# Starting the first supertile after eight of 24 modulation chunks, with the other 16 read beside its attention

## What is computed

```python
mod = c @ ada_w[l] + ada_b[l]                        # (B, 6D)
sh1, sc1, g1, sh2, sc2, g2 = jnp.split(mod, 6, axis=-1)
h = rmsnorm(x, norm1_g[l]) * (1.0 + sc1) + sh1       # needs sh1, sc1 alone
x = x + g1 * token_mixer(h, ...)                     # g1: after the mixer
h = rmsnorm(x, norm2_g[l]) * (1.0 + sc2) + sh2       # needs sh2, sc2
x = x + g2 * hier_moe(h, ...)
# in the mixer, compressed keys and values of 32-token blocks:
blocks = blocks + pos
kc = gelu(flat(blocks) @ w1 + b1) @ w2
```

## Time and profile before

| | |
|---|---|
| median of 3 runs | 6014.1 us (5986.19 to 6021.75) |
| the profiled execution | 5981.45 us |
| its slowest core's span (core 3) | 5979.9 us |
| spans of the 8 cores | 5889.1 to 5979.9 us |
| PE, DVE, ACT, POOL busy on core 3 | 66%, 41%, 34%, 16% |

### The profile page before, as it was taken

How to read it: one execution, slowest core, us unless ns; L and a number is a source line. 1 busy time by engine, 2 the same in 40 slices (tenths; PEclk the granted TensorE clock), 3 DMA queues, 4 the chain that set the end, 5 groups by cost and what they waited for, 6 DMA issues and landing times.

```text
span 5979.9 us, 101776 instructions; the slowest of 8 cores (5889.1 to 5979.9 us)
## 1 busy us (share of the span) xinstructions
PE 3965.3 (66%) x35620; PEld 2453.9 (41%) x35620; DVE 2446.7 (41%) x5534; ACT 2025.3 (34%) x3831; POOL 929.0 (16%) x876
## 2 busy tenths in 40 slices
PE   2477686775777766778687687865289998981000
PEld 1234353343444433344343344432167777771000
DVE  1245444364454444445445445533222222323444
ACT  0234344333354532435443244551011111112332
POOL 2001101011111001101100011001122333322222
PEclk9778778787787877878888778877599999995555
DMA  9567565556755456466564643212265545557886
GB/s 166 135 132 153 112 134 101 127 138 121 124 112 113 116 131 134 106 135 126 107 128 126 130 110 92 71 61 58 81 225 196 203 169 194 186 190 219 250 249 214
DMA packets 212104, 848.33 MB, mean 142 GB/s; under 512 B 37197, under 2 KB 42829, under 8 KB 198808
## 3 DMA queue, kind: packets, MB, share of 16 engines
q1 hardware_dynamic: 147960, 603.37, 32.2%
q0 software_dynamic: 63648, 238.47, 23.5%
HBM read 1218.00 MB, written 285.00 MB: 251 GB/s over the span
## 4 chain that ended last, share of the span: by engine, by line
PE 53%; DMA 17%; DVE 13%; issue 6%; POOL 5%; ACT 4%; another core or an unknown queue 1%; DVEq 1%; ACTq 0%; SPq 0%; POOLq 0%
PE bank L290 45%; DMA ring_u<-wst 8%; DMA xg_u<-h2s,gidu_u 5%; PE bank L293 3%; POOL wl_u L308 3%; PE ACCA L290 2%; DVE wl_u L311 2%; PE ACCB L290 2%; DMA ring_u<-ada_wc 2%; DMA ring_u<-wch 1%; DVE wl_u L308 1%; ACT wl_u L296 1%; POOL h2t_u L308 1%; DVE tmp_u L308 1%
## 5 line engine op out<-in xcount | busy, mean ns | idle before, releaser
L290 PE MATMUL bank<-h1T_u,ring_u 128*128 128x512 bf16 x3072 | 956.8, 420 | 435.6 <-DMA ring_u<-wst 390.1
L296 ACT ACTIVATE pe_u<-bank 128x512 bf16<-128x512 f32 x1648 | 950.5, 598 | 660.1 <-PE ACCB L290 305.5
L290 PE MATMUL bank<-xT_u,wl_u 128*128 128x128 bf16 x10368 | 632.6, 224 | 1.0 <-issue 0.6
L290 PEld LDWEIGHTS bank<-xT_u,wl_u 128*128 128x128 bf16 x10368 | 613.6, 101 | 1.7 <-issue 1.4
L290 PEld LDWEIGHTS bank<-h1T_u,ring_u 128*128 128x128 bf16 x3072 | 297.1, 107 | 718.9 <-issue 548.5
L308 POOL TENSOR_TENSOR rv_u<-rv_u,mhalf_u 128x1 f32<-128x1 f32 x128 | 84.1, 661 | 2920.0 <-DVE rv_u L305 2919.9
L290 PE MATMUL bank<-qz_u,ksr_u 128*128 128x512 bf16 x1088 | 469.5, 432 | 15.8 <-ACT pe_u L296 15.8
L290 PEld LDWEIGHTS ACCA<-vsr_u,pe_u 128*128 128x128 bf16 x4352 | 313.6, 108 | 263.6 <-issue 107.8
L290 PE MATMUL bank<-wores_u,mixT_u 128*128 128x512 bf16 x1024 | 362.1, 418 | 70.1 <-DVE tmp_u L308 43.0
L308 DVE TENSOR_TENSOR he_u<-sg_u,bank 128x512 bf16<-128x512 bf16 x162 | 111.3, 687 | 633.3 <-PE bank L290 556.9
L290 PE MATMUL ACCA<-vsr_u,pe_u 128*128 128x65 bf16 x4352 | 346.0, 206 | 12.0 <-ACT osel_u L299 5.1
(11 more groups left out here) (269 smaller groups left out, 6417.4 us busy)
## 6 DMA issues: line engine op xcount, KB each, us to landing
wl_u<-wsc SPq DMA_DIRECT2D x162, 3072.0 KB
ring_u<-wst SPq DMA_DIRECT2D x390, 512.0 KB
wsc<-exp_all POOLq DMA_DIRECT2D x64, 1536.0 KB, 18.9
wl_u<-yks SPq DMA_DIRECT2D x128, 512.0 KB, 7.8
xs_u<-x SPq DMA_DIRECT2D x64, 512.0 KB
x_u<-x SPq DMA_DIRECT2D x64, 512.0 KB
x1s<-x_u SPq DMA_DIRECT2D x64, 512.0 KB, 3.0
wl_u<-x1s SPq DMA_DIRECT2D x64, 512.0 KB, 6.3
```

The source lines that it names most:

```text
L290: P.emit('pe', lambda e: e.matmul(out, lhsT, rhs, start=start, stop=stop, skip_group_check=True), rd, wr)
L296: P.emit('act', lambda e: e.activation(out=out, in_=in_, func=func, **kw), rd, wr)
```

## The change

The head now ends after the constants that eight modulation chunks need; the rest moves.

- **Head.** DVE clears first. POOL loads `cT`, `identb` and the four ring slots; SP loads the first two x tiles and its constants. Then the barrier, which leaves out the ring slots and the x tiles. Behind it POOL issues 25 loads: 11 constants, four pieces of `vcaug`, and the rows of `ksr` in ten pieces where there were two. Then follow modulation chunks 0 to 7 and `d1(0)`.
- **`biasc`.** The eight `w1` chunks are no longer read for it alone. In `d1(0)` their matmuls with `posT` stand beside the compression ones, in `bank3`.
- **`modgen`** is a new generator woven with `d1(1)` in phase 0. Its first step issues the four `wores` loads (POOL), the copy of `ebase`, the clearing of `fill` and the 18 stores to `idt` (SP); then come modulation chunks 8 to 23, one to a step, all in `bank3`, through the same ring.
- Four small tiles stay allocated, and the x loads of `d1(0)` are no longer issued behind the barrier.

```diff
-    def barrier(self):
+    def barrier(self, skip=()):
...
+                if s in skip:
+                    continue
...
-            for q in range(4):
-                DMA('pool', wores[q][:], wch_d[27 + q][:, 0:2048], 'cst_pool', (), [wores[q]])
...
-            DMA('pool', ksr[0][64:128, :], e40_d, 'cst_pool', (), [ksr[0]])
-            DMA('pool', ksr[1][0:64, :], e40_d, 'cst_pool', (), [ksr[1]])
-            MS(fill[:], PAD, fill)
-            nfill = ROWS // 128
-            for f in range(nfill):
-                DMA('sp', idt_d[f * 128:(f + 1) * 128, :], fill[:], 'fill', [fill], [('idt', 'fill', f)])
+            DMA('pool', cT[:], cT_d, 'l_cT', (), [cT])
+            DMA('pool', identb[:], identf_d, 'l_idb', (), [identb])
+            for c in range(NR):
+                R.warm(c)
+            for q in range(2):
+                DMA('sp', xs[q][:], x_d[q * 128:q * 128 + 128, :], f'xl{q}', (), [xs[q]])
...
+            P.barrier(skip=[f'ring{i}' for i in range(NR)] + ['xl0', 'xl1'])
+            late = [(posT, posT_d), (ptcur, ptcur_d), (ptfirst, ptfirst_d), (ptprev, ptprev_d), (poolw, poolw_d), (w2sb, w2r_d),
+                    (maskD, maskD_d), (maskW, maskW_d), (selvalid, selv_d), (selbiasc, selb_d), (tri, tri_d)]
+            for n_, (dst, src) in enumerate(late):
+                DMA('pool', dst[:], src, f'lt{n_}', (), [dst])
+            for p in range(2):
+                for g in range(2):
+                    DMA('pool', vcaug[p][:, g, 64:97], ovl_d, f'lo{p}{g}', (), [vcaug[p]])
+            for m in range(5):
+                o_ = m * 512
+                DMA('pool', ksr[0][64:128, o_:o_ + 512], e40_d[:, o_:o_ + 512], f'le0{m}', (), [('ks', 0, m)])
+                DMA('pool', ksr[1][0:64, o_:o_ + 512], e40_d[:, o_:o_ + 512], f'le1{m}', (), [('ks', 1, m)])
...
+            def modgen():
                 for q in range(4):
-                    ci, w = R.get(adac(8 + q4 * 4 + q))
...
+                    DMA('pool', wores[q][:], wch_d[27 + q][:, 0:2048], f'lw{q}', (), [wores[q]])
+                P.emit('dve', lambda e: e.tensor_copy(out=base[1][:, 4, :], in_=ebase[:]), [ebase], [base[1]])
+                MS(fill[:], PAD, fill)
+                for f in range(ROWS // 128):
+                    DMA('sp', idt_d[f * 128:(f + 1) * 128, :], fill[:], 'fill', [fill], [('idt', 'fill', f)])
+                bk = banks[3]
+                for q4 in range(4):
+                    mr, br = mrow[q4 % 2], brw[q4 % 2]
+                    DMA('sp', br, adabr_d[:, q4 * D:(q4 + 1) * D], f'brwl{q4 % 2}', (), [br])
+                    for q in range(4):
+                        ci, w = R.get(adac(8 + q4 * 4 + q))
+                        wv = V3(w[:, 0:2048], 8)
+                        for k in range(8):
+                            MM(bk[0:nseq, 0:256], cT[:, k, :], wv[:, k, :], start=(k == 0), stop=(k == 7), rd=[w, cT], wr=[bk])
+                        R.done(ci)
+                        cs = slice(q * 256, q * 256 + 256)
+                        TT(mr[:, cs], bk[0:nseq, 0:256], br[:, cs], ALU.add, rd=[bk, br], wr=[mr])
+                        yield 1.0
...
+                    DMA('sp', mod_d[:, q4 * D:(q4 + 1) * D], mr, f'modst{q4 % 2}', [mr], [('mod_d', q4)])
...
-            for kv in range(2):
-                bk = PS()
-                for qd in range(4):
-                    ci, w = R.get(plainchunk(wch_d[7 + 4 * kv + qd], 2048))
...
-            P.barrier()
-            pp.close()
...
+                            if si == 0:
+                                for cc in range(2):
+                                    MM(banks[3][:, cc:cc + 1], wv[0:64, l8, cc * 128:(cc + 1) * 128], posT[0:64, kv, l:l + 1],
+                                       start=(l == 0 and cc == 0), stop=(l == 31), rd=[w, posT], wr=[banks[3]])
...
-            for q in range(2):
-                d1_load(0, q)
             solo(d1(0, False))
...
+                if ph_ == 0:
+                    xy.append(modgen())
```

More of the change, by code:

```diff
@@ L429, in phase_a @@
             R.slots = ring
-            pp = ExitStack()
-            adabT = sb("adabT_s", [128, 48], F32, pp)
-            n1g = sb("n1g_s", [128, 8], F32, pp)
-            posT = sb("posT_s", [128, 2, 32], BF16, pp)
-            b1T = sb("b1T_s", [128, 2, 2], F32, pp)
+            adabT = a("adabT_s", [128, 48], F32)
+            n1g = a("n1g_s", [128, 8], F32)
+            posT = a("posT_s", [128, 2, 32], BF16)
+            b1T = a("b1T_s", [128, 2, 2], F32)
             fill = tmp[:, 0:128]
@@ L462, in phase_a @@
                     MS(vcaug[p][:, g, 0:64], 0.0, vcaug[p])
-            DMA('pool', identb[:], identf_d, 'cst_pool', (), [identb])
-            for p in range(2):
-                for g in range(2):
-                    DMA('pool', vcaug[p][:, g, 64:97], ovl_d, 'cst_pool', (), [vcaug[p]])
             for t in [hidv, kcT, vcT, ucarry, selb, kwr[0], kwr[1], qzs[0][0], qzs[0][1], qzs[1][0], qzs[1][1],
@@ L495, in phase_a @@
             TT(s1T[:], s1T[:], n1g[:].unsqueeze(2).broadcast_to([128, 8, nseq]), ALU.mult, rd=[s1T, n1g], wr=[s1T])
-            for q4 in range(4):
-                mr, br = mrow[q4 % 2], brw[q4 % 2]
-                DMA('sp', br, adabr_d[:, q4 * D:(q4 + 1) * D], f'brwl{q4 % 2}', (), [br])
+            TS(w2sb[:], w2sb[:], 0.5, None, ALU.mult, rd=[w2sb], wr=[w2sb])
+            def modgen():
                 for q in range(4):
-                    ci, w = R.get(adac(8 + q4 * 4 + q))
-                    wv = V3(w[:, 0:2048], 8)
-                    bk = PS()
-                    for k in range(8):
-                        MM(bk[0:nseq, 0:256], cT[:, k, :], wv[:, k, :], start=(k == 0), stop=(k == 7), rd=[w, cT], wr=[bk])
-                    R.done(ci)
-                    cs = slice(q * 256, q * 256 + 256)
-                    TT(mr[:, cs], bk[0:nseq, 0:256], br[:, cs], ALU.add, rd=[bk, br], wr=[mr])
-                if q4 == 0:
-                    TS(mr, mr, 0.5, None, ALU.mult, rd=[mr], wr=[mr])
-                if q4 == 2:
-                    TS(mr, mr, 1.0, None, ALU.add, rd=[mr], wr=[mr])
-                    TT(mr, mr, n2row, ALU.mult, rd=[mr, n2row], wr=[mr])
-                DMA('sp', mod_d[:, q4 * D:(q4 + 1) * D], mr, f'modst{q4 % 2}', [mr], [('mod_d', q4)])
@@ L514, in phase_a @@
-            MODK = [('mod_d', q) for q in range(4)]
-            for kv in range(2):
-                bk = PS()
-                for qd in range(4):
-                    ci, w = R.get(plainchunk(wch_d[7 + 4 * kv + qd], 2048))
-                    wv = V3(w[:, 0:2048], 8)
-                    for l8 in range(8):
-                        for cc in range(2):
-                            l = qd * 8 + l8
-                            MM(bk[:, cc:cc + 1], wv[0:64, l8, cc * 128:(cc + 1) * 128], posT[0:64, kv, l:l + 1],
-                               start=(l == 0 and cc == 0), stop=(l == 31), rd=[w, posT], wr=[bk])
-                    R.done(ci)
-                TT(biasc[:, kv, :], bk[:, 0:2], b1T[:, kv, :], ALU.add, rd=[bk, b1T], wr=[biasc])
+                    DMA('pool', wores[q][:], wch_d[27 + q][:, 0:2048], f'lw{q}', (), [wores[q]])
@@ new lines, in modgen @@
+                P.emit('dve', lambda e: e.tensor_copy(out=base[1][:, 4, :], in_=ebase[:]), [ebase], [base[1]])
[15 more added lines that the diff above has]
+                        yield 1.0
+                    if q4 == 0:
+                        TS(mr, mr, 0.5, None, ALU.mult, rd=[mr], wr=[mr])
+                    if q4 == 2:
+                        TS(mr, mr, 1.0, None, ALU.add, rd=[mr], wr=[mr])
+                        TT(mr, mr, n2row, ALU.mult, rd=[mr, n2row], wr=[mr])
+                    DMA('sp', mod_d[:, q4 * D:(q4 + 1) * D], mr, f'modst{q4 % 2}', [mr], [('mod_d', q4)])
```

22 lines of the change are left out of this document (6 added, 16 removed).

## The result

The changed kernel took 5995.2 us (median of all 9 runs), the kernel before beside it 6015.0 us (9 runs). The ratio is 0.990, with a 95% interval of 0.985 to 0.995: 61 us faster, between 33 and 90. In some executions of any of these kernels the cores of one die run longer at a lower granted clock, and this ratio and the later ones leave those out (4 of the 9 of the changed kernel, 2 of the 9 before; the others have means of 5950.0 and 6011.2 us). The forecast was 48 us.

A forecast was written before the change was run, and what follows sets the result against it. The prediction took the head to be bound by the DMA engines alone. Its terms, -100 + 21 + 18 + 7 + 6 = -48 us, took 6014.1 us to 5966 us, with a range of 5908 to 6012 us.

The forecast's parts named there:

- Term A: Head, up to the first projection of d1(0): -100 us, with bounds of 88 and 106 us gained.
- Term B: Rest of d1(0): 0 us; 4.5 us if the load no longer covers the added posT matmuls.
- Term C: Start of phase 0 to first projection of d1(1): +21 us from waits behind the 18 stores; bounds +3 to +32.
- D: Ten modulation chunks among the projections of phase 0: +18 us of matmuls, bounds 5 and 26.
- E: Bias rows of the last two groups in phase 0, where DVE stops: +7 us, between 0 and 12.
- F: Ring in phase 0, now bringing 31 chunks through four slots instead of 15: +6 us, bounds 0 and 20.
- The rule that I weighed there: DMA engines alternate queues by packet, so SP's table crawls beside wores: start of phase 0 +32 us, sum -37 us.
- The waits are cheap: Rival: stores issued in 0.35 us, most of ten chunks in PE's idle time: -86 us, 5928 us; chance 0.32.
- Given back: Rival: smaller head gain and larger costs in phase 0 leave -8 us, 6006 us; chance 0.12.
- Every moved chunk becomes a wait: Rival: each of 16 chunks stands open 10.3 us on PE and DVE: +65 us, 6079 us; chance 0.03.
- It doesn't do what it says: Rival: the change fails its intent, for instance because the barrier still waits for the ring; given nothing.

The follow-up runs named there:

- e4: Changed kernel with one common semaphore for the two vcaug loads of a tile; first projection of d1(0) 5.9 us earlier, phase 1 4.7 us earlier.
- e6: Changed kernel with the second x pair of d1(0) loaded with the first, ahead of the barrier; first projection 8.8 us earlier, phase 1 8.5 us earlier.
- e5: Kernel before with only the w1 pass dropped and its posT matmuls put in d1(0); first projection 23.2 us earlier, phase 1 19.5, phase 2 11.1.
- e3: Changed kernel with the four wores loads moved behind modulation chunk 23; phase 1 9.7 us earlier, phase 2 5.3 us later.
- e9: Changed kernel with one matmul instead of eight for modulation chunks 8 to 23; first projection of d1(1) to phase 1 took 101.8 us, against 109.4.
- e7: Changed kernel with modgen run alone between d1(0) and phase 0, not woven; phase 1 began at 376.7 us, against 338.6 changed and 380.2 before.
- e10: Changed kernel with all mends (early bias rows and x tiles, spread stores and wores, shared vcaug semaphores), second run; 0.982 of before, median 5994.2 us.
- e2: Changed kernel with the clearing of fill and the 18 table stores moved behind modulation chunk 23; phase 1 18.2 us earlier, phase 2 12.2 us earlier.

## Why the prediction was right, and where its terms were off

The time lies inside the range and 13 us from the forecast of -48; at the marks it is -41.6 on the mean core and 382.7 - 335.2 = -47.6 on core 3. Sign, size and mechanism hold: the head was bound by the DMA engines, the change took 88 us out of it, and the start of phase 0 gave part back. That the sum on core 3 is within 1 us of the forecast is luck: its terms are off by 12, 1.5, 15 and 25 us, and cancel. On core 3:

| term | predicted | measured |
|---|---|---|
| A, to z0 | -100 | -88.1 |
| B, `d1(0)` | 0 | -1.5 |
| C, S to z1 | +21 | +35.6 |
| D, E and F, z1 to P1 | +18, +7, +6 | +6.4 |

The parts that the prediction names for its range (91 us gained at one end, 8 at the other, and 28 us below and 8 above for the runs) would give 5895 to 6014 us; the stated 5908 to 6012 is a little narrower, which decides nothing here.

**Term A**, its pessimistic bound of 88. The barrier opened at 23.4 us, when the last constant landed, and not at 21, when DVE had cleared its tiles. The 25 issues were priced at 0.58 us each, which is right for one (44.3 - 23.8 = 20.5 us, less 7.5 of waits, is 0.52 each), but two of the `vcaug` loads wait for another load into the same tile to land. The earlier trace rows show four of them in 2.30 us without a wait, and the diff shows the new semaphore names; I read the first and not the second. e4 showed it to be worth 5.9 us. Chunk 4 took 8.8 us from the start of its issue (7.5 taken), and from its use on, the chain kept its step: it was 10.1 us late there and 10.3 at the last store (76.7 against 66.4). The x pair was ready 7.2 us after its issue, not 4.6, which I put down to the stores and ring loads that drain beside it. e6 showed what this queue place costs in all: 8.8 us.

**Term B** held. In the mean of the cores S-z0 grew from 65.7 to 67.7 us, and to 68.4 in e5, where in `d1(0)` only the `biasc` matmuls were added; both are under the 4.5 us of the bound.

**Term C** failed at two steps. The first is the stores: 1.14 us each by the earlier trace rows, where ring loads and `wores` ran beside them too (the four `wores` loads were issued from 10.1 us on and landed in 26.4), but 1.54 us here, 27.8 in place of 20.5. e3 showed how much hangs on that traffic (0.91 us each without `wores`). The bias row's own time was 4.2 us, not 5.6. So it was ready at S+34.7, not at S+28.7: 6.0 us. The larger part, 9.0 us, is behind it, from the bias row to z1: 34.7 us where I had 25.7. I let the path go through the second x pair, 4.6 us from its issue to its norm, and took the attention's order as it was. It was 14.3 us, and not for the load: in order on ACT stands the copy of the first pair's `h1T`, and in order on PE, ahead of that pair's last transposes, matmuls of the attention with a wait of 3.4 us for a selection. ACT and PE had been standing for 25 and 32 us: a stop of DVE stops the other two with it, and they start again one behind the other. From that norm to z1 it was 18.3 us, where I had 17.1 with the bias row; it holds 2.6 us for the row and, right ahead of z1, the 4.4 us for the second selection. The two selections are 7.8 us of waits on PE where before had one of 3.0. By their places ahead of the last transposes and of z1 I put 4.8 of the 9 us down to this, a change of the order by the weaving that the sum leaves out; no run undoes it alone. It isn't the matmuls of the six chunks (e9). The rest of the 9 us no run took apart.

The rule that I weighed there, from the Trainium skill ("DMA: Bandwidth & Descriptors", section "Queues, rings and completion order"), put the bias row at S+40.0 (16.9 us behind the stores, at their 1.14 us). It came at S+34.7, half way between the rule and my value. The trace agrees with the rule in direction, small rows go slower beside the large ones of `wores`, but shows it at another place: in longer issues of the stores on SP, while the row behind them then landed in 4.2 us.

**Terms D, E and F** gave +6.4 us, not +31 (+8.4 in the mean of the cores, from which the following is). D was 14.8 us less the 3.6 that came back, about 11, not 18. I priced eight matmuls at 1.86 us in the head and scaled them up to 2.6 by the mean clock; in the trace of after they take from 1.03 to 1.87 us and never more. And I expected part of them to lie in PE's idle time: none does, but the other work ran faster beside them. F has its size: 5.4 us of waits for chunk loads, 6 forecast. E is small: DVE waits 2.4 us for one of the two bias rows on core 3 and not for the other. What made the sum so much smaller is a term that it leaves out: 7.8 us of the attention, matmuls and a wait, went ahead of z1 and so into C.

**The rivals.** *The waits are cheap* was refuted at the stores (1.54 us each, not 0.35), and it had +10 us for D, E and F, near the +6.4, but by chunks in PE's idle time, where none lies. *Given back* was nearest in A and C (88 and 32) and far off in D, E and F. *Every moved chunk becomes a wait* needed 6.3 us of open wait for each; the ten among the projections have 3.8 us together on core 3. e7 gives the other end: alone the part costs 81 us, nearly as much as the 87 that the change takes out of the head, so the change lives by the 37.5 us that the weaving hides. *It doesn't do what it says*: PE began its first chunk in the moment the barrier opened.

## What to carry to other kernels

Before work is moved out of a head that the DMA engines bind, list what stands behind it in each queue at its new place: here 1.2 MB that nobody needed soon stood ahead of one 16 KB row and one pair of x tiles on which two engines waited, and that cost 19 of the 87 us gained by z0. Loads that nobody needs soon belong a few at a time behind steps that run anyway (e10, where this came together with the other mends and wasn't tried by itself), and neither at the first nor at the last step, where e2 and e3 gave back part of what they won. And a second load into a tile under another semaphore is a wait for the first one's landing, which no count of issues shows. Third, a generator more in a weave moves the others against each other: before two stretches are compared by their busy times, count their instructions.
